# float32r products with their moving operand read and written backwards, and weight parts interleaved element by element

## The reference, cut to what matters

```python
# first block
z = rmsnorm(x, norm1_g) @ w_in                     # 1024 -> 7184 columns
ya = conformer_conv(a_val, a_gate, ...)            # ends in @ w_conv_out
yb = forgetting_attention(q, k, v, c) @ w_fox_out
x = x + (sigmoid(g_a) * ya + sigmoid(g_b) * yb) @ w_out
x = x + peer_ffn(rmsnorm(x, norm2_g), ...)         # 16384 experts: h @ peer_u.T, gates, @ peer_v
# second block
z = rms_norm(x, norm_mix) @ w_in_2;  mk, mv = rms_norm(mem) @ w_mem_kv
merged = sum over three branches of sigmoid(z_gate) * (branch @ w_branch)
x = x + merged @ w_out_2
up = causal_dwconv(rms_norm(x, norm_ffn) @ w_up, ...)
x = x + (gelu(gate_h) * val_h) @ w_down
```

## Time and profile before

| | us |
|---|---|
| runs, median of 2 | 1597.63 (1597.41 to 1597.86) |
| span of the profiled execution | 1595.2 |
| PE busy | 1583.0 |
| PEld (weight loads) busy | 1493.5 |
| DVE busy | 1071.3 |
| ACT busy | 884.2 |
| POOL busy | 885.8 |

### The profile page before, as it was taken

One profiled execution on the slowest core, in us unless ns is written; L12 is line 12 of the kernel. 1 busy time (PEld: TensorE's weight loads), 2 busy tenths in 40 slices (PEclk: granted clock), 3 DMA queues, 4 the chain that ended last, 5 costly groups with the idle time before them and its releaser, 6 DMA issues.

```text
span 1595.2 us, 33476 instructions
## 1 busy us (share of the span) xinstructions
PE 1583.0 (99%) x12568; PEld 1493.5 (94%) x12568; DVE 1071.3 (67%) x1867; ACT 884.2 (55%) x1251; POOL 885.8 (56%) x413
## 2 busy tenths in 40 slices
PE   9999999999999999999999999999999999999998
PEld 8999899999999999998888888889999999999998
DVE  7998643779933777778888666776937383455521
ACT  6557766454454444444444445457676654666653
POOL 8786468868886000000000244457876689888886
PEclk9999999999999999999999999999999999999999
DMA  6565346555555555555555666666543356666653
GB/s 222 171 191 154 106 132 187 186 175 190 188 184 186 171 171 171 172 169 171 179 178 166 215 190 194 195 189 185 172 148 106 109 177 185 188 190 187 191 187 119
DMA packets 86218, 277.03 MB, mean 174 GB/s; under 512 B 11233, under 2 KB 18161, under 8 KB 86129
## 3 DMA queue, kind: packets, MB, share of 16 engines
q1 hardware_dynamic: 85712, 274.76, 54.9%
q0 software_dynamic: 272, 1.05, 0.2%
q10 hardware_dynamic: 144, 0.00, 0.0%
HBM read 274.73 MB, written 1.05 MB: 173 GB/s over the span
## 4 chain that ended last, share of the span: by engine, by line
PE 93%; issue 2%; DVE 2%; POOL 1%; ACT 1%; DMA 0%; SPq 0%; DVEq 0%; ACTq 0%; POOLq 0%
PE gemm L679 36%; PE gemm L982 22%; PE gemm L684 18%; PE aux L1268 4%; PE gemm L813 3%; PE aux L962 2%; POOL w_lo L462 1%; PE gemm L700 1%; PE gemm L725 1%; PE gemm L1268 1%; PE aux L932 0%; PE gemm L799 0%; ACT w_hi L1364 0%; PE gemm L706 0%; PE gemm L742 0%
## 5 line engine op out<-in xcount | busy, mean ns | idle before, releaser
L462 POOL TENSOR_TENSOR w_lo<-raw,w_hi 128x1024 fp32r<-128x1024 f32 (+1 forms) x330 | 791.7, 2407 | 294.7 <-ACT w_hi L1364 285.6
L1364 ACT ACTIVATE w_hi<-raw 128x1024 fp32r<-128x1024 f32 (+1 forms) x492 | 515.8, 1050 | 575.5 <-PE gemm L679 324.0
L679 PE MATMUL gemm<-h_lo,w_hi 128*128 128x256 f32 x2144 | 294.3, 279 | 0.0
L679 PE MATMUL gemm<-h_hi,w_hi 128*128 128x256 f32 x2096 | 293.3, 282 | 0.4 <-ACT w_hi L1364 0.3
L684 PE MATMUL gemm<-h_hi,w_lo 128*128 128x256 f32 x2096 | 288.6, 280 | 1.4 <-POOL w_lo L462 0.9
L679 PEld LDWEIGHTS gemm<-h_lo,w_hi 128*128 128x128 f32 x2144 | 268.9, 188 | 0.3 <-issue 0.2
L679 PEld LDWEIGHTS gemm<-h_hi,w_hi 128*128 128x128 f32 x2096 | 264.0, 188 | 3.3 <-issue 1.6
L462 DVE TENSOR_TENSOR w_lo<-raw,w_hi 128x1024 fp32r<-128x1024 f32 x162 | 196.6, 1222 | 104.3 <-ACT w_hi L1364 103.7
L684 PEld LDWEIGHTS gemm<-h_hi,w_lo 128*128 128x128 f32 x2096 | 262.8, 188 | 3.5 <-POOL w_lo L462 2.2
L982 PE MATMUL gemm<-w_hi,act_parts 128*128 128x512 f32 x1008 | 250.9, 391 | 0.4 <-ACT act_parts L1565 0.4
L982 PEld LDWEIGHTS gemm<-w_hi,act_parts 128*128 128x128 f32 x1008 | 188.0, 188 | 39.0 <-issue 0.5
(11 more groups left out here) (436 smaller groups left out, 2065.6 us busy)
## 6 DMA issues: line engine op xcount, KB each, us to landing
raw<-in_w_u SPq DMA_DIRECT2D x128, 512.0 KB, 3.6
raw<-in_w_ev SPq DMA_DIRECT2D x128, 512.0 KB, 3.7
raw<-in_w_up SPq DMA_DIRECT2D x48, 512.0 KB, 4.3
raw<-in_w_gate SPq DMA_DIRECT2D x24, 512.0 KB, 3.8
raw<-in_w_down SPq DMA_DIRECT2D x24, 512.0 KB, 4.0
raw<-in_w_conv_in SPq DMA_DIRECT2D x16, 512.0 KB, 4.6
raw<-in_w_peer_q SPq DMA_DIRECT2D x16, 512.0 KB, 3.5
raw<-in_w_branch SPq DMA_DIRECT2D x24, 288.0 KB, 2.9
```

What stands on the lines that cost most here:

```text
L462: eng.tensor_tensor(w_lo[v][:, 0:n], raw[c.raw][v][:, 0:n], w_hi[v][:, 0:n], ALU.subtract).then_inc(lo_ready[v], 1)
L679: mm = pe.matmul(out, w[:, k, :], act_part[:, k, :], start=(n == k == 0), stop=False)
L1364: act.activation(w_hi[v][:, 0:n], raw[c.raw][v][:, 0:n], ACT.Copy).then_inc(hi_ready[v], 1)
```

## The change

`w_hi` and `w_lo` become two interleaved views of one tensor: element n of the hi part lies at 2n and that of the lo part at 2n + 1. Every view of them in the kernel (by ScalarE, the subtracting engine and TensorE) therefore steps two elements (8 bytes). And in every float32r product the moving operand and the output are read and written from the last column to the first; the result in PSUM is the same. The stationary operand is given as before, in forward order. Number, order and sizes of the instructions, waits and transfers stay.

```diff
-        w_hi = [sb(f"w_hi{v}", [P, TILE], F32R) for v in range(2)]
-        w_lo = [sb(f"w_lo{v}", [P, TILE], F32R) for v in range(2)]
+        w_parts = [sb(f"w_parts{v}", [P, TILE, 2], F32R) for v in range(2)]
+        w_hi, w_lo = [[w_parts[v][:, :, part] for v in range(2)] for part in range(2)]
...
+        def back(tile):
+
+            return tile[:, ::-1]
+
...
-                        mm = pe.matmul(out, w[:, k, :], act_part[:, k, :], start=(n == k == 0), stop=False)
+                        mm = pe.matmul(back(out), w[:, k, :], back(act_part[:, k, :]), start=(n == k == 0), stop=False)
...
-                    mm = pe.matmul(out, w[:, k, :], x[0][:, k, :], start=False, stop=(k == steps - 1))
+                    mm = pe.matmul(back(out), w[:, k, :], back(x[0][:, k, :]), start=False, stop=(k == steps - 1))
...
-                            mm = pe.matmul(pair(gemm[c.bank])[:, tt, :],
-                                           x[:, v * KD // 2 + k, tt * P:(tt + 1) * P], w[:, k, :],
+                            mm = pe.matmul(back(pair(gemm[c.bank])[:, tt, :]),
+                                           x[:, v * KD // 2 + k, tt * P:(tt + 1) * P], back(w[:, k, :]),
...
-                                mm = pe.matmul(gemm[2 * half + tt][:, :], a[:, c.raw, v, tt * P:(tt + 1) * P],
-                                               w[v][:, half * (D // 2):(half + 1) * (D // 2)],
+                                mm = pe.matmul(back(gemm[2 * half + tt]), a[:, c.raw, v, tt * P:(tt + 1) * P],
+                                               back(w[v][:, half * (D // 2):(half + 1) * (D // 2)]),
...
-                            mm = pe.matmul(out, w[v][:, k * P:(k + 1) * P], x[:, g * KD + k, :],
+                            mm = pe.matmul(back(out), w[v][:, k * P:(k + 1) * P], back(x[:, g * KD + k, :]),
```

More of the change, by code:

```diff
@@ L699, in high @@
                         pe.wait_ge(hi_ready[v], c.split + 1)
-                    pe.matmul(both[:, v, :], hi[v][:, k, :], x[0][:, k, :], start=(v == k == 0), stop=False,
+                    pe.matmul(back(both[:, v, :]), hi[v][:, k, :], back(x[0][:, k, :]), start=(v == k == 0), stop=False,
                               skip_group_check=True)
@@ L705, in low @@
                         pe.wait_ge(lo_ready[0], c.split + 1)
-                    return pe.matmul(both[:, 0, :], lo[:, k, :], x[0][:, k, :], start=False, stop=False,
+                    return pe.matmul(back(both[:, 0, :]), lo[:, k, :], back(x[0][:, k, :]), start=False, stop=False,
                                      skip_group_check=True)
@@ L724, in paced_product @@
                             pe.wait_ge(split, before + k // step + 1)
-                        mm = pe.matmul(both[:, v, :], hi[v][:, k, :], x[1][:, k, :], start=False,
+                        mm = pe.matmul(back(both[:, v, :]), hi[v][:, k, :], back(x[1][:, k, :]), start=False,
                                        stop=(v == 0 and k == KD - 1), skip_group_check=True)
@@ L730, in paced_product @@
                 for k in range(KD):
-                    mm = pe.matmul(both[:, 1, :], lo[:, k, :], x[0][:, k, :], start=False, stop=(k == KD - 1),
+                    mm = pe.matmul(back(both[:, 1, :]), lo[:, k, :], back(x[0][:, k, :]), start=False, stop=(k == KD - 1),
                                    skip_group_check=True)
@@ L741, in part @@
                     for k in (2 * g, 2 * g + 1):
-                        mm = pe.matmul(both[:, v, :], w[v][:, k, :], x[:, k, :], start=(begins and k == 0),
+                        mm = pe.matmul(back(both[:, v, :]), w[v][:, k, :], back(x[:, k, :]), start=(begins and k == 0),
                                        stop=(ends and k == KD - 1), skip_group_check=True)
@@ L1009, in one @@
                     def one(w, a, half, tt, ends=False):
-                        return pe.matmul(gemm[2 * half + tt][:, :], a[:, c.raw, v, tt * P:(tt + 1) * P],
-                                         w[v][:, half * (D // 2):(half + 1) * (D // 2)], start=False, stop=ends,
+                        return pe.matmul(back(gemm[2 * half + tt]), a[:, c.raw, v, tt * P:(tt + 1) * P],
+                                         back(w[v][:, half * (D // 2):(half + 1) * (D // 2)]), start=False, stop=ends,
                                          skip_group_check=True)
```

## The result

The changed kernel takes 2041.39 us (2041.21 to 2041.57) where the kernel before takes 1597.63: a ratio of 1.278, 95% interval 1.274 to 1.282. It is 443.8 us slower. The forecast was 1543 us with a range up to 1625; what came is the second rival, the stepped stream, 119 us above the 1922 us that stood there.

A forecast was written before the change was run, and what follows sets the result against it. The prediction took PE's matmul count times start-to-start distance as the bound: span 1595.2 - 54.6 (stationary products) + 0 (moving weights) + 0 (splitting) = 1540.6, plus 2.4 us median offset, giving 1543 us; range 1502 to 1625.

The forecast's parts named there:

- the second rival, the stepped stream: In ev and by_token, the stepped moving stream loses rate; at half rate the kernel takes 1922 us; chance 0.09.
- What bounds the kernel: On PE, the number of matmuls times the distance between starts sets the end; PE busy 1583.0 of 1595.2 us.
- Rest as collisions of load and stream: All float32r matmuls: the 10 to 13.4 ns above the bare stream are weight load and moving stream colliding in SBUF.
- Stationary products, 54.6 us gained: 8832 matmuls with stationary weights fall to 111 ns each: 36 us gained with h tiles, 18.5 with others.
- the idea: In SBUF, interleaving matches load and stream speeds; reversal aligns or parts their directions; readers moving together stop colliding.
- The 111 ns: Expected distance per stationary-weight matmul, from float32 keys at 111.6 ns and float16 gate planes scaled to 110.6.
- Products with moving weights: ev and by_token: 0 taken, between 26 us gained and 27 lost; 379 us lost if a stepped stream takes twice its time.
- Two accesses per line: SBUF reads: a stride is free with at least two accesses per 16-byte line, so the 379 us loss doesn't occur.
- The splitting: ACT, POOL and DVE writing the weight parts: 0 taken; 290 us lost if POOL takes 1.5 times its time.
- Transfers: Weight transfers: 512 KB per 2.66 us need 197 GB/s, slices reach 222 and 215, so nothing waits.
- 262 ns in ev: Distance per ev matmul beyond which the stepped stream's loss outweighs the gain elsewhere.
- the 55 us: Gain elsewhere, from the stationary products, subtracted from the 379 us loss when pricing the slower stream at 1922 us.

The follow-up runs named there:

- p2: Probe of the kernel before, loads in u and up varied: 64-column load 118.8 ns per matmul (plain 116.3), load stepping 8 bytes 120, stepping 16 bytes 234.
- p1: Probe of the kernel before, ev streams and float16 gate planes read by other patterns: 8-byte step 448 ns forward, 465 backward, spaced pairs 452, plain 230.
- p3: Probe of the kernel before, other ev stream patterns: 256 elements twice each 215 ns, one element 512 times 220, 256 columns at 16 bytes 230, at 12 bytes 225.
- e4: Kernel before without the unused floats beside h, so h lies 32 bytes lower: 1616.72 us, ratio 1.0112.
- p4: Probe of the kernel before, loads in u and up beginning at other offsets within the weight tile: 1606.94 us; 120 or 118 ns per matmul by offset.
- p6: Probe of the kernel before, streams in u and up beginning 16 to 256 bytes further into the h tiles: 1602.0 us; 117 to 120 ns per matmul.
- e1: Kernel before with weight parts interleaved by single elements, nothing reversed: 2026.93 us.
- p5: Probe of the kernel before, ev streams in rows of neighbours, gate planes at other float16 steps: rows of 4 230 ns, of 2 340; float16 at 16 bytes 118.
- e2: Kernel before with moving operand and output reversed, weight parts not interleaved: 1612.67 us, ratio 1.0084.
- e7: Kernel before with weight parts interleaved in blocks of 128 elements, nothing reversed: 1599.42 us, ratio 0.9997.

## Why the prediction was wrong

- *What bounds the kernel.* Right: matmuls times distance, before and after.
- *Rest as collisions of load and stream.* Wrong in the main, and the root of the forecast. A half load saves nothing (p2), a stepped stream costs the same per unit as a plain one (p1), and reading each element twice removes most of the rest with the load unchanged (p3). A float32r stream without steps takes its data at 1.77 ns per 16 bytes, 4 columns, where the array would take them in 1.67. That is 7 of the 10 to 12 ns at 256 columns and all of the 13 at 512. The 1.7 ns between h and x tiles, from which I argued, are real and depend on addresses (e4, p4, p6), but they are a second effect.
- *Stationary products, 54.6 us gained.* Wrong in sign: 19 us lost. The stepped load costs h products 4 ns with plain order (e1), and the reversal regains 0.6 to 1 of it. In down it costs 1.7 and the reversal regains 2.2, which leaves 0.5 gained; so the direction does count, as the idea had it, but for 2 ns and not 7. The 111 ns rested on two rows of other kinds. That of the keys, 111.6 ns for 128 columns in plain float32, shows no overlap that a float32r stream lacks: in the same trace 256 such columns take 216 ns beside a load of only 16 (L799), so that 128 of them are 108 ns by themselves.
- *Products with moving weights, taken as 0 between 26 gained and 27 lost, with 379 as the upper end.* This is the step that decided. The upper end came, and more: 425 us. I chose against it by L962, whose step is two elements, and let "two elements" stand for the 8 bytes of this change though I had noted that there they are 4. Four columns of L962 lie in 16 bytes, as in a plain float32r stream; that is why it showed no loss. Float16 steps of 8 bytes (p1), and of 6, 12 and 16 (p5), do slow down. The excess over 379, which stands for 440 ns in ev, has two halves: the stepped stream takes 1.77 ns per unit and not 1.67 (455 ns, e1), and the reversal, which costs a plain stream 7 ns, costs a stepped one 13 (467.7). A small slip: twice the rest is 26 us lost by the same products, not 27.
- *Two accesses per line.* By the Trainium skill, "SBUF — State Buffer", section "Door 1: The DMA port swizzle", two accesses per 16-byte line are enough for full bandwidth. The unit of 16 bytes is what p1 and p5 show; the rule for the stride is not: two float32r columns per unit run at half the rate (467.7 against 226.7 ns), three at 230 ns for 384 columns (p5), and only four keep it. The measurement decides. The Trainium skill's PSUM rule ("PSUM — Partial Sum Buffer", "Specifications (TRN2)"), that any non-contiguous pattern slows matmuls significantly, isn't borne out for a reversed output: 233.5 against 227 ns in e2, and even that may come from the stream read backwards, since no run reverses the output alone.
- *The splitting.* Nearly right: 2% on POOL where I took nothing, 13% on ACT, and PE's waits for either stay at 1 us or less at each line.
- *Transfers.* Right, PE waited for none.
- *The rivals.* The second, at 0.09, came. The decisive point that I had set, 262 ns in ev, was the right test. Its price was 119 us too low: 46 of that in the moving products, as above, and 74 because the 55 us set off against it as gained elsewhere were 19 lost. The chance was too low: the doubled stream was a bound that I had worked out myself, and only an analogy of another step in bytes stood against it.

## What to carry to other kernels

Count the 16-byte units of SBUF that a float32r moving operand touches, not its columns: where a partition's row is read with fewer than four float32 to a unit, the rate of the matmul falls in proportion, down to half. If two parts must share a tensor, interleave them by what one matmul reads: blocks of 512 bytes cost nothing (e7). Rows of 16 bytes kept the stream's rate in p5, but begun at element 0 of the tile, and what they would cost the load and the splitting wasn't measured. And when a row of the trace is taken as an analogue, compare in the unit that the hardware could count, bytes here, and not in the unit of the program.

## What was not expected of the hardware

- A plain float32r stream is itself limited, by all signs by its fetching: 227 ns for 512 columns, 215 when each element is used twice (p3).
- Reading backwards costs 3% of a stream of 512 (233.5 against 227 ns, e2), and nearly as much again where the stream steps 8 bytes (467.7 against 455, after and e1).
- A float32r stream read forward has a ceiling of 0.85 to 0.89 ns per column at steps of 8, 12, 16, 32 and 64 bytes (p1, p3, p7); float16 at 16 bytes takes 1.8 (p5), and so does a load at 16 bytes (p2).
- 32 bytes in the place of a tensor change the whole kernel by 1.1% (e4).
- A load of 128 columns may step 8 bytes for 4 ns a matmul beside h tiles and 1.7 in down (e1), and for nothing in down where the stream is reversed (117.8 ns with and without the step); at 16 bytes it doubles the matmul's time (234 ns, p2).
